# Hybrid diffusion backbone: gate and up weights of the first layer's experts as 128x128 blocks, and seven places for that layer's expert weights

## The reference, cut to what matters

```python
def ec_moe(h, w_router, w_e_gate, w_e_up, w_e_down):
    cap = EC_CAPACITY * t // N_EXPERTS
    aff = softmax(h @ w_router)
    vals, idx = top_k(swapaxes(aff, 1, 2), cap)
    xs = h[idx]
    hid = silu(xs @ w_e_gate) * (xs @ w_e_up)      # 1024 -> 1408
    ys = (hid @ w_e_down) * vals                   # 1408 -> 1024
    return zeros.at[idx].add(ys)
```

## Time and profile before

| | us |
|---|---|
| median of 3 runs | 3601.54 (3598.33 to 3605.52) |
| the profiled execution | 3597.66 |
| its span | 3595.9 |
| first layer ahead of its experts | 0 to 1195 |
| experts of the first layer | 1195 to 2001 |
| second layer ahead of its experts | 2001 to 2911 |
| experts of the second layer | 2911 to 3596 |

### The profile page before, as it was taken

One profiled execution on the slowest core, in us unless ns is written; L12 is line 12 of the kernel. 1 busy time (PEld: TensorE's weight loads), 2 busy tenths in 40 slices (PEclk: granted clock), 3 DMA queues, 4 the chain that ended last, 5 costly groups with the idle time before them and its releaser, 6 DMA issues.

```text
span 3595.9 us, 74576 instructions
## 1 busy us (share of the span) xinstructions
PE 3397.3 (94%) x32464; PEld 2343.4 (65%) x32464; DVE 1170.0 (33%) x2535; ACT 707.2 (20%) x1346; POOL 99.8 (3%) x171
## 2 busy tenths in 40 slices
PE   7899999999999999999999989899999999999998
PEld 4456757678764777777677656667677565555554
DVE  1443415336624211111111362415265242222222
ACT  3313321122322000000001432321132201111111
POOL 0000100000000000000000000100000000000000
PEclk9999999999999999999999999999999999999999
DMA  5512120020034999999999501220211269999995
GB/s 219 221 51 71 35 82 12 30 71 34 27 129 200 352 367 356 362 366 375 347 358 345 185 31 44 70 82 13 82 45 53 110 262 420 423 419 418 420 421 244
DMA packets 104784, 732.84 MB, mean 204 GB/s; under 512 B 8464, under 2 KB 14864, under 8 KB 61472
## 3 DMA queue, kind: packets, MB, share of 16 engines
q1 hardware_dynamic: 95120, 692.54, 48.7%
q0 software_dynamic: 9360, 35.71, 3.5%
HBM read 706.15 MB, written 16.83 MB: 201 GB/s over the span
## 4 chain that ended last, share of the span: by engine, by line
PE 78%; DMA 9%; DVE 7%; ACT 3%; issue 3%; DVEq 0%; POOL 0%; ACTq 0%; SPq 0%; POOLq 0%
PE psum L709 14%; PE psum L1308 10%; PE psum L1299 8%; PE psum L1337 8%; PE psum L599 8%; PE psum L592 5%; PE psum L1162 4%; PE psum L711 3%; DMA ring<-in_w_e_gate 3%; DMA ring<-in_w_ada 2%; DMA ring<-in_w_e_down 2%; PE psum L1343 2%; PE psum L1353 2%; PE psum L576 2%; DVE work L2045 2%
## 5 line engine op out<-in xcount | busy, mean ns | idle before, releaser
L709 PE MATMUL psum<-HT,ring 128*128 128x256 f32 x2560 | 599.3, 388 | 13.9 <-DVEq L2298 5.3
L709 PEld LDWEIGHTS psum<-HT,ring 128*128 128x128 f32 x2560 | 487.7, 194 | 97.8 <-issue 21.3
L1308 PE MATMUL psum<-work,ring 128*64 128x96 f32 x11264 | 486.4, 248 | 42.5 <-issue 33.1
L1308 PEld LDWEIGHTS psum<-work,ring 128*64 128x64 f32 x11264 | 473.0, 138 | 59.7 <-issue 49.7
L1528 ACT ACTIVATE work<-psum,small 128x768 f32<-128x768 f32 (+4 forms) x208 | 146.1, 703 | 682.7 <-PE psum L1343 323.1
L599 PE MATMUL psum<-ring,HT 128*128 128x512 f32 (+1 forms) x768 | 276.0, 521 | 0.0
L1337 PE MATMUL psum<-ring,work 128*64 128x512 f32 x1056 | 240.6, 597 | 6.4 <-DMA ring<-in_w_e_down 6.3
L1531 ACT ACTIVATE work<-psum 128x256 f32<-128x256 f32 (+7 forms) x219 | 103.5, 473 | 696.1 <-PE psum L1322 259.1
L599 PEld LDWEIGHTS psum<-ring,HT 128*128 128x128 f32 x768 | 145.8, 190 | 127.3 <-issue 120.5
L592 PE MATMUL psum<-HT,ring 128*128 128x256 f32 (+3 forms) x624 | 192.8, 470 | 0.3 <-issue 0.3
L1299 PE MATMUL psum<-ring,work 128*64 128x256 f32 x768 | 173.7, 381 | 0.0
(11 more groups left out here) (249 smaller groups left out, 4021.0 us busy)
## 6 DMA issues: line engine op xcount, KB each, us to landing
ring<-in_w_e_gate SPq DMA_DIRECT2D x48, 2048.0 KB, 10.8
ring<-in_w_e_up SPq DMA_DIRECT2D x48, 2048.0 KB, 11.4
ring<-in_w_e_down SPq DMA_DIRECT2D x48, 2048.0 KB, 10.2
ring<-in_w_ada SPq DMA_DIRECT2D x24, 2048.0 KB, 12.7
ring<-in_w_e_gate SPq DMA_DIRECT2D x24, 1536.0 KB, 9.4
ring<-in_w_e_up SPq DMA_DIRECT2D x24, 1536.0 KB, 9.6
ring<-in_w_e_down SPq DMA_DIRECT2D x24, 1536.0 KB, 10.2
ring<-in_w_gate SPq DMA_DIRECT2D x16, 2048.0 KB, 8.8
```

What stands on the lines that cost most here:

```text
L709: pe.matmul(b[:, 0:256], w[:, k, d4 * P:(d4 + 1) * P], HT[:, k, off:off + 256], start=(k == 0), stop=(k == KD - 1))
L1308: ins = pe.matmul(b[lo:lo + 64, f * cap:(f + 1) * cap], w[k][:, c0:c0 + 64], e_xs[:, k, 0:cap], start=(k == 0), stop=(k == KD - 1))
```

## The change

- `gate_up` in the first layer issues one matmul for a block of 128 weight columns, where there were two of 64. The result covers all 128 PSUM partitions at once. The number of L1308's records falls from 11264 to 5632.
- The first layer's pieces go round seven places: `ht`, `ht_yt`, `yt`, `xn`, and the three slots. `yt` is the rest of `YT`, `xn` is `work[:, 0:4096]`. In the last expert the list leaves out `yt`.
- Piece 0 now waits for the router (`aff`), for the stored zeros and for the stored rows; piece 4, the first in a slot, waits for `rows_in`; the `pack` load goes with piece 9.
- `early_diag[0]` moves to `X[:, 2048:4096]`, since its old area is in `xn`.
- The second layer's piece numbers shift by two, so that its first piece (`mla0`) goes to the slot that is free earliest.

```diff
-    N_IN.append(N_EXP[_L] + 0)
+    N_IN.append(N_EXP[_L] + 2)
-HOMES = [["r0", "r1", "r2"],
+HOMES = [["r0", "r1", "r2", "ht", "ht_yt", "yt", "xn"],
          ["r0", "r1", "r2", "ht", "ht_yt", "low"]]
...
     if L == 0:
-        cycle = [f"r{(N_EXP[0] + i) % SLOTS}" for i in range(SLOTS)]
-        return cycle[q % SLOTS]
+        cycle = ["ht", "ht_yt", "yt", "xn"] + [f"r{(N_EXP[0] + i) % SLOTS}" for i in range(SLOTS)]
+        if q < (NE - 1) * PIECES_EXP:
+            return cycle[q % len(cycle)]
+        return [home for home in cycle * 3 if home != "yt"][q - (NE - 1) * PIECES_EXP + (NE - 1) * PIECES_EXP % len(cycle)]
...
-        early_diag = [area(0, 2048).rearrange("p (j k c) -> p j k c", j=2, k=KD),
+        early_diag = [xr[:, 2048:4096].rearrange("p (j k c) -> p j k c", j=2, k=KD),
...
                                 for k in range(KD):
-                                    for half in range(2):
-                                        lo, c0 = 64 * half, f * P + 64 * half
-                                        ins = pe.matmul(b[lo:lo + 64, f * cap:(f + 1) * cap], w[k][:, c0:c0 + 64], e_xs[:, k, 0:cap],
-                                                        start=(k == 0), stop=(k == KD - 1))
+                                    ins = pe.matmul(b[:, f * cap:(f + 1) * cap], w[k][:, f * P:(f + 1) * P], e_xs[:, k, 0:cap],
+                                                    start=(k == 0), stop=(k == KD - 1))
...
-                    if L == 0 and q == 2:
+                    if L == 0 and q == 0:
+                        sp.wait_ge(sems["aff"], 1)
+                        sp.wait_ge(sems["zeroed"], 16)
+                        sp.wait_ge(sems["xn_stored"], 16 * len(qtiles(0)))
+                    elif L == 0 and q == 4:
                         sp.wait_ge(sems["rows_in"], 16)
-                    elif L == 0 and q == 3:
-                        sp.wait_ge(sems["aff"], 1)
+                    elif L == 0 and q == PIECES_EXP:
                         sp.dma_start(packs[:, :], I["pack"][1]).then_inc(sems["pack_in"], 16)
```

More of the change, by code:

```diff
@@ L269, in hybrid_layers @@
         ht_ = HT.rearrange("p k t -> p (k t)")
-        PLACE = {"r0": (run(0, SLOT),), "r1": (run(1, SLOT),), "r2": (run(2, SLOT),), "ht": (ht_[:, 0:4096],), "ht_yt": (ht_[:, 4096:6144], YTr[:, 0:2048]), "low": (work[:, 0:2048], work[:, 8192:10240])}
+        PLACE = {"r0": (run(0, SLOT),), "r1": (run(1, SLOT),), "r2": (run(2, SLOT),), "ht": (ht_[:, 0:4096],), "ht_yt": (ht_[:, 4096:6144], YTr[:, 0:2048]), "yt": (YTr[:, 2048:6144],), "xn": (work[:, 0:4096],), "low": (work[:, 0:2048], work[:, 8192:10240])}
         def piece_parts(L, q):
@@ L485, in hybrid_layers @@
         e_row = xr[:, 0:2048].rearrange("p (j n) -> p j n", j=2)
-        e_diag = xr[:, 2048:4096].rearrange("p (j k c) -> p j k c", j=2, k=KD)
         facc = YTr.rearrange("p (t d) -> p t d", t=NT)
```

## The result

| | before | changed |
|---|---|---|
| median, us | 3603.53 | 3695.97 |
| lowest to highest | 3598.33 to 3605.65 | 3691.96 to 3699.56 |
| profiled execution | 3597.66 | 3694.27 |
| its span | 3595.9 | 3692.5 |

The changed kernel is slower: ratio 1.0258, 95% interval 1.0241 to 1.0276, or +92 us between medians. The prediction said 3718 (3690 to 3755).

The account below looks back on a forecast made before the run. The prediction took PE's own work to bound the first layer's experts, with a smaller loss to full DMA queues. Blocks +165.6, idle time -47 and start +1 gave +119.6 us, so 3718 us, range 3690 to 3755.

Parts of the forecast that it names:

- The stage and its bound: First layer's experts: bound by PE's own work (94%), a smaller part lost to full DMA queues; grows to about 926 us.
- The blocks, +165.6 us: Gate and up, first layer: 5632 full-width records step at 112 ns, set by the weight load, against 82.6 a pair.
- The idle time, -47 us: First layer's experts: of PE's 51 us idle, 47 go and 4 stay; bounds -51 and -14.5.
- What takes it away: First layer's experts: places remove 14.5 us of weight waits; fewer instruction fetches and less full queues remove 32 us.
- -14.5 if the issue gaps stay: First layer's experts: smallest idle-time gain, if only PE's waits for weights go.
- The start, +1 us: Start of the first layer's experts: up to 8 MB of pieces beside the first gather, not 4; bounds 0 and +5.
- Edits at nothing: Moved `early_diag`, earlier `mla0` load, `down` and the whole second layer: no cost or gain.
- rival 1: Gate and up: load hides behind the stream, step stays at 82.6 ns or rises little; 3555 us; chance 5%.
- rival 2: Gate and up: load as short as that of transpose L1268, step 90.6 ns; 3600 us, no change; chance 2%.
- Rival 3: First layer's experts: idle time stays, fetches and gathers still queue behind 2 MB pieces; 3753 us; chance 7%.
- Rival 4: Gate and up: PE's clock falls, at half clock the step doubles, 631 us more; about 4350 us; chance 1%.

Follow-up runs that it names:

- The blocks alone: Kernel before with only the full-width 128x128 gate and up matmuls, still three slots; 3692.30 us, ratio 1.0272 to the kernel before.
- the places alone: Changed kernel with gate and up put back to halves of 64 columns, seven places kept; 3596.78 us, ratio 1.0007 to the kernel before.

## Why the prediction was right or wrong, point by point

**The whole.** The direction and the term that decides it were right. The time was 22 us too high. The measured 3696 lies under the forecast's own range (3700 to 3749) and inside only the wider 3690 to 3755, whose lower end had no reason of its own, so that the range holds it is partly luck. With the step as measured and all idle time gone, the prediction's sum still gives 3601 + 163.9 - 50 + 1 = 3716, so the idle-time term was off by more than its own bound.

**The stage and its bound.** Right: everything happened in the first layer's experts, and PE sets them.

**The blocks, +165.6 us.** Right in mechanism and size. The step was 111.7 ns (112 taken), so the term is 5632 x (111.7 - 82.6) = 163.9 us. The line from 96, 112 and 128 weight columns shows that it is the load; the unchanged step with 64 moving columns shows that it isn't the stream. Of the two rules on the Trainium skill's page "TensorE: Matmul & The Clock Gate" that the prediction names, columns over 1.2 GHz for a load (section "LDWEIGHTS (loading the stationary operand)") holds (0.83 ns a column, with 5 ns on top that the page doesn't give). The other, the step from the moving columns alone, doesn't hold where the stream is shorter than the load. The prediction took it for more than it is. The section that gives it ("Back-to-back issue gap") says as well that in a stream of loads and matmuls both set the spacing. This case agrees, with 111.7 ns where the moving columns alone would make it 82.6.

**The idle time, -47 us.** This is the term that was mis-sized, and the 96.9 us by which the stage really grew (804.81 us from the first gate matmul to the end of `down`, then 901.75) gives its true size: 163.9 - 96.9 = 67 us. I had bounded it at 51, the idle time. But a record of L1308 counts as busy for 246 ns, while a pair comes every 82.6. So each gap hides its first part in "busy", and L1308's 486.4 us held 21 us more than 5632 x 82.6 = 465.2. The changed kernel's 636.43 hold 7 more than its 629, with no gaps, so 14 of the 21 are loss. These 14 and 51.35 - 0.73 = 50.6 us less idle time make 65 of the 67; the last 2 aren't placed. The measure that shows such loss is the undisturbed step, not idle time. (By the medians, which lie 92.4 us apart, the term is some 72 us.)

**What takes it away.** That the issue gaps are fetches of PE's instructions was right: they stand at one place of 256. But my reason for their going was wrong in part. I gave 14.5 us to the places and 32 to fewer fetches and emptier queues. The blocks alone took all of it, in three slots, and the places alone took none. The waits for weights and the issue gaps aren't two sums to subtract: without the one, the other grew from 33.1 to 46.0 us. My lower bound for this term, "-14.5 if the issue gaps stay", was no bound at all.

**The start, +1 us.** Measured 0.9, with a wait for the rows that is 3.7 us longer and a PE that came 2.3 us sooner.

**Edits at nothing.** Right: the second layer's two stretches are 910.00 and 684.50 us long, against 910 and 685.

**The rivals.** The hidden load (rival 1) and the short load of L1268's kind (rival 2) fell to the step and to the 192 ns of the load. Rival 3 fell too: 0.73 us of idle time. Rival 4, the clock, didn't happen: the stage has 1.00. But the changed kernel with 64 moving columns was granted 0.73 over the stage in the one execution that it had, so the 1%, which rested on one window of 2 us, looks low. At a clock of 0.50 its step was 213 ns, near the doubling that the rival assumed.

## What to carry to other kernels

A float32 matmul with 128 weight columns stepped no faster than its load, 112 ns, with 96 moving columns and with 64. Two halves of 64 side by side load in about half the time (a pair every 58.7 ns), so at 96 columns they win, 82.6 against 111.7 ns. By the 0.84 ns a moving column of the earlier trace rows the two would meet near 130 columns; that is an estimate. Look for loss in the undisturbed step times the number of instructions, since idle time and "busy" both leave some of it out. When a buffer takes one wait away and nothing gets faster, find what else was late by nearly as much: here it was the fetch of PE's instructions, and only a PE order that spreads the short ones made the seven places worth 34 us.

## What the runs showed of the hardware

- The load of a float32 block: 111.7, 98.3 and 85.0 ns a step for 128, 112 and 96 weight columns, and 58.7 ns for two of 64 side by side (with 64 moving columns).
- The granted clock fell to 0.50 while PE was never idle: with 128 weight and 64 moving columns it went up and down through the stage, and the kernel took 3999.62 us in its one execution, 304 us more than with 96 moving columns. With 96 the stage had 1.00.
- One packet of the instruction queue, 16 KB, brings 256 of PE's instructions. All 260 gaps that the profile calls "issue" in gate and up, in the eight kernels of the table, stand at the same place of 256. In the kernel before they are 0.2 to 3.4 us long and 33.1 us in all.
- These gaps all but went (4.7 us) when DMA brought half of the bytes (0.67 share), and went also when the records were 40% fewer at a DMA share of 1.00.
- A change from half-width to full-width matmuls costs some 175 ns, and the change back 143 ns.
